# Scores and value products of the differential attention layer: from full fp32 products to three rounded ones

## What is computed

```python
def _diff_attention(cols, ...):          # 4 heads, two query/key halves of 128 features each
    qh = cols[..., :1024].reshape(b, seq, 4, 2, 128) * 128 ** -0.5
    kh = cols[..., 1024:2048].reshape(b, seq, 4, 2, 128)
    v = heads(cols[..., 2048:], 4, 256)
    for i in range(seq // 128):
        end = (i + 1) * 128
        def probs(qq, kk):
            s = einsum('bhqd,bhkd->bhqk', qq[:, :, i * 128:end], kk[:, :, :end]) + bias
            return softmax(where(mask, s, -inf))
        a = probs(q1, k1) - lam * probs(q2, k2)
        outs.append(einsum('bhqk,bhkd->bhqd', a, v[:, :, :end]))
```

## Time and profile before

| what | us |
|---|---|
| median of 3 runs (lowest, highest) | 3045.61 (3045.04, 3046.34) |
| the profiled execution, its time | 3048.35 |
| its span | 3046.6 |
| TensorE matmuls busy in the span | 3007.6 |
| VectorE busy | 2082.2 |
| ScalarE busy | 1388.7 |
| GpSimd busy | 50.6 |
| mean granted TensorE clock | 0.999 of full |

### The profile page before, as it was taken

The page is one execution under the profiler, slowest core; times in us unless marked ns, Lnnn a source line. Parts: engine busy times, 40 slices in busy tenths (PEclk is TensorE's granted clock), DMA queues, the critical chain, the costliest instruction groups (busy, mean ns, idle before and its releaser), DMA issues.

```text
span 3046.6 us, 45649 instructions
## 1 busy us (share of the span) xinstructions
PE 3007.6 (99%) x18093; PEld 2647.9 (87%) x18093; DVE 2082.2 (68%) x2423; ACT 1388.7 (46%) x1852; POOL 50.6 (2%) x148
## 2 busy tenths in 40 slices
PE   9999999999999999999999999999999999999998
PEld 8878998888888998888889988788998888889987
DVE  6987885566557876566578764656885556578854
ACT  3475553444335553344355543324553443345534
POOL 5100000000000000000000000000000000000000
PEclk9999999999999999999999999999999999999999
DMA  5122332342123333211223332223332222133322
GB/s 173 57 60 89 110 119 95 102 141 70 53 87 97 106 101 104 90 56 60 93 97 110 97 103 90 91 70 102 110 105 96 91 83 65 62 107 99 110 90 77
DMA packets 250549, 283.30 MB, mean 93 GB/s; under 512 B 11874, under 2 KB 216864, under 8 KB 250408
## 3 DMA queue, kind: packets, MB, share of 16 engines
q1 hardware_dynamic: 250408, 281.30, 28.8%
HBM read 279.16 MB, written 4.73 MB: 93 GB/s over the span
## 4 chain that ended last, share of the span: by engine, by line
PE 89%; DVE 6%; ACT 2%; issue 2%; POOL 1%; DMA 0%; SPq 0%; DVEq 0%; ACTq 0%
PE ps L2568 28%; PE ps L2203 17%; PE ps L2205 16%; PE ps L2204 16%; PE ps L2838 1%; PE ps L2840 1%; PE ps L2839 1%; PE ps L2752 1%; ACT whi L752 1%; DVE wlo L1321 1%; PE ps L2760 1%; PE ps L2819 1%; PE ps L2798 1%; PE ps L2695 1%; PE ps L2715 1%
## 5 line engine op out<-in xcount | busy, mean ns | idle before, releaser
L752 ACT ACTIVATE whi<-raw 128x2048 fp32r<-128x2048 f32 (+2 forms) x184 | 323.2, 1756 | 729.4 <-PE ps L2205 672.2
L1321 DVE TENSOR_TENSOR wlo<-raw,whi 128x2048 fp32r<-128x2048 f32 (+1 forms) x179 | 373.6, 2087 | 346.9 <-ACT whi L752 346.3
L2203 PE MATMUL ps<-hh,whi 128*128 128x512 f32 x1056 | 421.6, 399 | 0.0
L2568 PE MATMUL ps<-th,wh 128*128 128x256 f32 x1440 | 408.7, 284 | 7.3 <-ACT us L849 3.9
L2205 PE MATMUL ps<-hh,wlo 128*128 128x512 f32 x1056 | 412.0, 390 | 0.0
L2204 PE MATMUL ps<-hl,whi 128*128 128x512 f32 x1056 | 411.6, 390 | 0.0
L2568 PE MATMUL ps<-tl,wh 128*128 128x256 f32 x1440 | 407.5, 283 | 0.0
L2568 PE MATMUL ps<-th,wl 128*128 128x256 f32 x1440 | 407.4, 283 | 0.0
L2203 PE MATMUL ps<-ringh,whi 128*128 128x512 f32 x860 | 335.4, 390 | 7.5 <-issue 6.0
L2204 PE MATMUL ps<-ringl,whi 128*128 128x512 f32 x860 | 334.7, 389 | 0.0
L2205 PE MATMUL ps<-ringh,wlo 128*128 128x512 f32 x860 | 334.7, 389 | 0.0
(11 more groups left out here) (456 smaller groups left out, 5823.1 us busy)
## 6 DMA issues: line engine op xcount, KB each, us to landing
raw<-in_w_ffn_in SPq DMA_DIRECT2D x88, 1024.0 KB, 5.1
raw<-in_w_in SPq DMA_DIRECT2D x59, 1024.0 KB, 5.3
raw<-in_w_ffn_out SPq DMA_DIRECT2D x40, 1024.0 KB, 5.1
raw<-in_w_o SPq DMA_DIRECT2D x32, 640.0 KB, 4.1
raw<-in_w_gate SPq DMA_DIRECT2D x11, 1024.0 KB, 5.3
raw<-in_w_up SPq DMA_DIRECT2D x11, 1024.0 KB, 5.3
raw<-in_w_down SPq DMA_DIRECT2D x10, 1024.0 KB, 5.0
raw<-in_w_mem_kv SPq DMA_DIRECT2D x8, 1024.0 KB, 5.6
```

The costliest lines, as they stand in the source:

```text
L752: a.activation(whi[:, slot, 0:n], raw[:, slot, 0:n], ACT.Copy).then_inc(hi_made, 1)
L1321: v.tensor_tensor(wlo[:, u % 2, 0:n], raw[:, u % 2, 0:n], whi[:, u % 2, 0:n].bitcast(F32), ALU.subtract).then_inc(lo_made, 1)
L2203: mm(dst, wh, xh, start=first, stop=False, skip_group_check=True)
L2568: e = mm(bank(b, HALF), wgt[:, q, w], xx, start=start and k == 0 and m == 0, stop=k == KD // 2 - 1 and m == 2, skip_group_check=True)
```

## The change

Three things are changed.

1. Of the scores of each half, blocks 2 and 3 (384 and 512 columns) go through `three`; blocks 0 and 1 stay fp32. ScalarE makes the rounded parts of q and k (`dqk_hi`, two copies of 128x512) and VectorE the rests (`dqk_lo`, two subtractions of 128x512). Both stand at slot 2c - 2 from DZ[hd]: slot -2 for c = 0, and slot 0 for c = 1. In VectorE's program of slot 0 they stand behind the additions, maxima and negation of c = 0. TensorE waits for them (`qk_lo`) ahead of the scores.
2. Of the value products, key blocks 0 and 1 (512 and 384 columns) go through `three`. The values' first two blocks are split at slot 4 (ScalarE `dv_hi`, VectorE `dv_lo`, 512 elements a partition). At slot 5 ScalarE's one copy of 1280 columns becomes one of 384 (`dpt`) and one of 896 (`dpt_hi`), and VectorE subtracts 896 columns (`dpt_lo`) straight from PSUM. TensorE waits for `dpt_lo` and `dv_lo` ahead of the value products, and for `dpt_lo` ahead of the next head's scores.
3. Six semaphores that GpSimd sets in the first block become one, `pool_set`, with running counts. No instruction is added or removed by that.

The splits of c = 0 and the late ones lie in parts of act2's memory that are free then; those of c = 1 share dp[1]'s and dpt_hi's, so ScalarE's copies wait for the value products of the head before (`d_pv`).

```diff
@@ ScalarE, differential_slot
+                for c in range(2):
+                    for hd in at_slot(DZ, s, 2 * c - 2):
+                        act.wait_ge(acc_free, g_in(1) + evicted(2 + 3 * hd, c))
+                        act.wait_ge(S("m_tr"), 2 * MH)
+                        if hd:
+                            act.wait_ge(S("d_pv"), hd)
+                        for m, b in enumerate((qp, kp)):
+                            a.activation(dqk_hi[c][:, m, :], b[hd % 2][:, c, :], ACT.Copy).then_inc(S("qk_hi"), 1)
+                for hd in at_slot(DZ, s, 4):
+                    act.wait_ge(acc_free, g_in(1) + evicted(3 + 3 * hd, 0))
...
+                    a.activation(dv_hi[hd // 3][:, :, :], vp[hd % 2][:, 0:2, :], ACT.Copy).then_inc(S("dv_hi"), 1)
...
-                    a.activation(dpt[:, :], ps[:, 0:ZW], ACT.Copy).then_inc(S("d_pt"), 1)
+                    a.activation(dpt[:, :], ps[:, DWIDE:ZW], ACT.Copy).then_inc(S("d_pt"), 1)
+                    a.activation(dpt_hi[:, :], ps[:, 0:DWIDE], ACT.Copy).then_inc(S("d_pt"), 1)
@@ VectorE, differential_slot, behind the loop of L2028, L2032 and L2034
+                for c in range(2):
+                    for hd in at_slot(DZ, s, 2 * c - 2):
+                        for m, b in enumerate((qp, kp)):
+                            dve.wait_ge(S("qk_hi"), 2 * (NH2 + 2 * hd + c) + m + 1)
+                            v.tensor_tensor(dqk_lo[c][:, m, :], b[hd % 2][:, c, :], dqk_hi[c][:, m, :].bitcast(F32),
+                                            ALU.subtract).then_inc(S("qk_lo"), 1)
+                for hd in at_slot(DZ, s, 4):
+                    dve.wait_ge(S("dv_hi"), hd + 1)
+                    v.tensor_tensor(dv_lo[hd // 3][:, :, :], vp[hd % 2][:, 0:2, :], dv_hi[hd // 3][:, :, :].bitcast(F32),
+                                    ALU.subtract).then_inc(S("dv_lo"), 1)
+                for hd in at_slot(DZ, s, 5):
+                    dve.wait_ge(S("d_pt"), 2 * hd + 2)
+                    v.tensor_tensor(dpt_lo[hd // 3][:, :], ps[:, 0:DWIDE], dpt_hi[:, :].bitcast(F32), ALU.subtract).then_inc(S("d_ptl"), 1)
@@ TensorE, differential_slot: value products
-                    pe.wait_ge(S("d_pt"), hd + 1)
+                    pe.wait_ge(S("d_pt"), 2 * (hd + 1))
+                    pe.wait_ge(S("d_ptl"), hd + 1)
+                    pe.wait_ge(S("dv_lo"), hd + 1)
...
+                            if j < 2:
+                                three(dst, dv_hi[b][:, j, cs], dv_lo[b][:, j, cs], dpt_hi[:, keys], dpt_lo[b][:, keys], j == 0, False)
+                                continue
@@ TensorE, differential_slot: scores
+                        pe.wait_ge(S("qk_lo"), 2 * (NH2 + m + 1))
                         for i in (0, 2, 3, 1):
...
+                            if i > 1:
+                                three(dst, dqk_hi[c][:, 0, rows], dqk_lo[c][:, 0, rows], dqk_hi[c][:, 1, 0:wq(i)],
+                                      dqk_lo[c][:, 1, 0:wq(i)], i != 2, True)
+                                continue
@@ GpSimd, and its readers
-            g.memset(er[:, :, 0:1], 1.0).then_inc(S("angle_ready"), 1)
+            g.memset(er[:, :, 0:1], 1.0).then_inc(S("pool_set"), 1)
...
-                pe.wait_ge(S("t_zero"), 3)
+                pe.wait_ge(S("pool_set"), 29)
```

More of the change, by code:

```diff
@@ L429, in build @@
         dp = [at(f"dp{i}", TMP + 5120 * i, [P, ZW]) for i in range(2)]
-        dpt = at("dpt", TMP + 10240, [P, ZW])
+        DWIDE = ZK[3]
+        dpt_hi = at("dpt_hi", TMP + 10240, [P, DWIDE], F32R)
+        dpt = at("dpt", TMP + 10240 + 4 * DWIDE, [P, ZW - DWIDE])
+        LATE = [A0 + (4 + 2 * i) * 2 * T * 4 for i in range(2)]
+        dpt_lo = [at(f"dpt_lo{i}", LATE[i], [P, DWIDE], F32R) for i in range(2)]
+        dv_hi = [at(f"dv_hi{i}", LATE[i] + 3584, [P, 2, 256], F32R) for i in range(2)]
+        dv_lo = [at(f"dv_lo{i}", LATE[i] + 5632, [P, 2, 256], F32R) for i in range(2)]
+        dqk_hi, dqk_lo = ([at(f"dqk_{n}{c}", (LATE[1], TMP + 5120)[c] + 4096 * k, [P, 2, T], F32R) for c in range(2)]
+                          for k, n in enumerate(("hi", "lo")))
         osq = [at(f"osq{i}", TMP + 15360 + 2048 * i, [P, T]) for i in range(2)]
@@ L1222, in differential_slot @@
                 for c in range(2):
+                    for hd in at_slot(DZ, s, 2 * c - 2):
[7 more added lines that the diff above has]
+                    act.wait_ge(acc_free, g_in(1) + evicted(3 + 3 * hd, 0))
+                    act.wait_ge(S("m_pv"), 2 * MH)
+                    if hd:
+                        act.wait_ge(S("d_pv"), hd)
+                    if hd == 3:
+                        act.wait_ge(S("d_z"), 2 * hd + 1)
+                    a.activation(dv_hi[hd // 3][:, :, :], vp[hd % 2][:, 0:2, :], ACT.Copy).then_inc(S("dv_hi"), 1)
+                for c in range(2):
                     for hd in at_slot(DZ, s, 1 + c):
@@ L2795, in differential_slot @@
                     pe.wait_ge(acc_free, g0 + evicted(3 + 3 * hd, 1))
+                    b = hd // 3
                     for d in range(2):
                         for j in range(4):
-                            e = mm(bank(6 + d, T - P * j, P * j), vp[hd % 2][:, j, P * d:P * d + P],
-                                   dpt[:, ZK[j]:ZK[j] + wk(j)], start=j == 0, stop=j == 3, skip_group_check=True)
+                            dst, keys, cs = bank(6 + d, T - P * j, P * j), slice(ZK[j], ZK[j] + wk(j)), slice(P * d, P * d + P)
+                            if j < 2:
+                                three(dst, dv_hi[b][:, j, cs], dv_lo[b][:, j, cs], dpt_hi[:, keys], dpt_lo[b][:, keys], j == 0, False)
+                                continue
+                            e = mm(dst, vp[hd % 2][:, j, cs], dpt[:, ZK[j] - DWIDE:ZK[j] - DWIDE + wk(j)],
+                                   start=False, stop=j == 3, skip_group_check=True)
                     e.then_inc(S("d_pv"), 1)
@@ L2813, in differential_slot @@
                         elif hd:
-                            pe.wait_ge(S("d_pt"), hd)
+                            pe.wait_ge(S("d_pt"), 2 * hd)
+                            pe.wait_ge(S("d_ptl"), hd)
                         else:
@@ L2817, in differential_slot @@
                         pe.wait_ge(acc_free, g0 + evicted(2 + 3 * hd, c))
+                        pe.wait_ge(S("qk_lo"), 2 * (NH2 + m + 1))
                         for i in (0, 2, 3, 1):
-                            e = mm(ps[:, ZQ[i]:ZQ[i] + wq(i)], qp[hd % 2][:, c, P * i:P * i + P], kp[hd % 2][:, c, 0:wq(i)],
-                                   start=i != 2, stop=True, skip_group_check=True)
+                            dst, rows = ps[:, ZQ[i]:ZQ[i] + wq(i)], slice(P * i, P * i + P)
+                            if i > 1:
+                                three(dst, dqk_hi[c][:, 0, rows], dqk_lo[c][:, 0, rows], dqk_hi[c][:, 1, 0:wq(i)],
+                                      dqk_lo[c][:, 1, 0:wq(i)], i != 2, True)
+                                continue
+                            e = mm(dst, qp[hd % 2][:, c, rows], kp[hd % 2][:, c, 0:wq(i)], start=True, stop=True, skip_group_check=True)
                         e.then_inc(S("d_z"), 1)
```

34 lines of the change are left out of this document (17 added, 17 removed).

## The result

Over all runs the changed kernel takes 3058.55 us (median of 6, 3057.61 to 3062.15) and the kernel before 3046.8 (median of 6, 3045.04 to 3050.57). The ratio on record is 1.0036, with a 95% interval of 1.0026 to 1.0046 (it is not the quotient of these two medians, which lie 11.75 us or 0.39% apart): slower by 0.36%, some 11 us, where the prediction had 0.21% and a range that ended at 3056.5.

What follows compares the result with a forecast made beforehand. TensorE, busy 99% of the span, was taken as the bound. Gains, three costs and restarts summed as -4.6 + 8.6 + 1.25 + 0.7 + 0.45 = +6.4 us, giving a median of 3052.0 us (0.21% more), range 3048 to 3056.5.

Steps and rivals of the forecast that it cites:

- What bounds the kernel: TensorE, busy 99% of the span, has no slack: saved columns shorten the program, new waits lengthen it in full.
- Gains: TensorE's scores save 0.29 us in each of 8 blocks, value products 0.58 a head: -4.6 us in sum.
- Cost 1: Ahead of scores c = 1, TensorE waits 2.04 to 2.2 us a head for VectorE's late subtractions: +8.6 us.
- Cost 2: Ahead of value products, TensorE waits for dpt_lo: 0.25 us in head 0, 0.5 in heads 1 and 2; +1.25 us.
- Cost 3: At slot 6, ScalarE's copies for the next head delay the squares by 1.05 us, with 0.70 cover: +0.7 us.
- Restarts: TensorE's first product after each of nine new waits takes longer, 0.05 us each: +0.45 us.
- The clock: TensorE's granted clock was expected to stay at full behind the new waits, so the sum held no cost for it.
- Rival B: Idle times of 2.1 us drop TensorE's clock to 1.2 GHz at scores c = 1: 19 us more, 3071; chance 0.03.
- Rival A: VectorE's subtractions are ready in time at slot 1, so gains arrive without that wait: 3043.0 us; chance 0.1.
- Rival D: Value products alternate formats at a price and save nothing: 3054.3 us; chance 0.05.
- Rival C: VectorE's lateness at slot 5 reaches 1 us a head, and head 3's c = 0 is late: 3056.7; chance 0.12.
- gain bounds: Range for the summed savings in scores and value products: -2.3 to -5.5 us, value products saving 0 to 0.75 a head.

Runs made afterwards that it cites:

- e5: Changed kernel with squares, wlo and q's c = 1 subtraction reordered, k's ahead of maxima, next head's c = 0 subtractions behind addition of squares; 3046.0 us, ratio 0.9989.
- e1: Changed kernel with VectorE's two subtractions of c = 1 moved ahead of the maxima, behind the additions; 3051.04 us, ratio 1.001 to the kernel before.
- e11: Changed kernel with only wlo moved behind dv_lo and dpt_lo in slots 4 and 5 of heads 0 to 2; one run, 3056.73 us.
- e10: Changed kernel with only ScalarE's squares ahead of its copies and VectorE's addition of squares ahead of next head's subtractions and bias; one run, 3055.7 us.
- e4: Changed kernel with c = 1 subtractions ahead of maxima, squares and their addition moved up, wlo behind dv_lo and dpt_lo; 3049.76 us, ratio 1.0006.
- e2: Kernel before, products still fp32, plus two unused VectorE subtractions that TensorE waits for ahead of scores c = 1; 3061.43 us, ratio 1.0038.
- e3: Changed kernel with 18 unread TensorE transposes ahead of the wait for the subtraction of c = 1; 3057.38 us, ratio 1.0028 to the kernel before.
- e12: e5 with 14 unread TensorE transposes in the first block, ahead of head 2's scores; 3044.01 us, ratio 0.9986 to the kernel before.

## Why the prediction was wrong, point by point

**What bounds the kernel: right.** TensorE had no slack; what it was made to wait went into the time in full.

**Gains: right.** -4.6 us forecast; 0.29 a score block and 0.56 a head of value products measured in head 0, which makes -4.6 us. In e5 the stretch is 0.5 us longer than this gain and the waits left would give, so it may be a little less over all heads.

**Cost 1: the right place and size.** It had scores c = 1 come 6.78 us behind scores c = 0. They came 6.87 us behind in head 0 (1325.28 to 1332.15), where 4.64 was the undisturbed distance: 2.23 us against 2.14, over the four heads 8.8 against 8.6 us. VectorE's timeline of head 1 shows the order that does it:

```profile
1362.55 1.68 DVE L2053 TENSOR_TENSOR dp<-ps,dbias 128x128 f32<-128x128 f32 x4
1364.15 1.65 DVE L2057 TENSOR_REDUCE mx<-dp 128x1 f32<-128x128 f32 x4
1365.84 0.17 DVE L2059 TENSOR_SCALAR ngm<-mx 128x4 f32<-128x4 f32 x1
1365.92 0.68 DVE L2064 TENSOR_TENSOR dqk_lo<-qp,dqk_hi 128x512 fp32r<-128x512 f32 x1
1366.52 0.68 DVE L2064 TENSOR_TENSOR dqk_lo<-kp,dqk_hi 128x512 fp32r<-128x512 f32 x1
```

The last ends at 1367.20, and TensorE starts at 1367.35. e1 settles that this is the cause.

**Cost 2: a little too large.** 1.25 us forecast; the distance from turns to value products grew by 0.85 us in all (0.05, 0.25, 0.55 and 0), and e11 gives 0.9 back.

**Cost 3: too small by a factor of three, in part by a step left out.** 0.7 us forecast, 2.1 measured (0.8 in head 0, 1.2 in head 1, by the distances 7.46 and 7.74 from value products to the product over partitions, against 6.63 and 6.53 undisturbed, which is 7.19 and 7.08 before less 0.56). The prediction followed only ScalarE: squares 1.05 us later, cover 0.70. But on VectorE the next head's bias stands in the same slot ahead of the addition of squares, and it had been free because VectorE was waiting anyway. Now the rests hold it up. VectorE's timeline of head 1:

```profile
1391.06 0.69 DVE L2064 TENSOR_TENSOR dqk_lo<-qp,dqk_hi 128x512 fp32r<-128x512 f32 x1 [4.51 <-ACT dqk_hi L1237]
1391.67 0.68 DVE L2064 TENSOR_TENSOR dqk_lo<-kp,dqk_hi 128x512 fp32r<-128x512 f32 x1
1392.27 0.68 DVE L2038 SCALAR_TENSOR_TENSOR dbias<-dist,dneg 128x512 f32<-128x512 f32 x1
1392.99 0.69 DVE L2094 TENSOR_TENSOR osq<-osq,osq 128x512 f32<-128x512 f32 x1
```

and ScalarE's:

```profile
1391.45 1.07 ACT L1262 ACTIVATE osq<-ps 128x512 f32<-128x512 f32 x2
```

The squares end at 1392.52 and the addition starts at 1392.99: half a microsecond behind, and as much in head 0. So this step makes about 0.9 of the 2.1 us. The other 1.2 are ScalarE's lateness, which was itself forecast too small: in e10, which has the squares first, they start 4.02 and 4.04 us behind the value products, and in the changed kernel 5.18 and 5.46, so they are late by 1.2 and 1.4 us and not by 1.05. e10 moved both parts and got 1.9 us back; e4, which moved the squares and left the rests ahead of the addition, got nothing back. No run moved VectorE's part alone.

**Restarts** (0.45 us) were counted apart; the distances above hold them already.

**The clock: the step that failed.** The sum held falls at nothing; in the profiled execution two of the four long waits had one, 3.4 us in all. Rival B was given 3 in 100, against it "a wait of 1.49 us left the clock at full". Both halves of that were poor. The mechanism is real, as the changed kernel and e2 show, and e3 supports it. And that wait said little about others: it and a second one of 1.6 us in the feed-forward part have no fall behind them in any of the fourteen profiles, while the wait of 1.6 us in the first block had none in the profile of before and one in seven others. The price was also wrong, the other way: 4.7 us at each of four waits, where a fall costs 1.7 and only some waits have one. By the share seen since, as an estimate, it should have stood in the sum as 4 x 1.7 x 11/20 = 3.7 us, not beside it as 19 us at 3 in 100.

The sum in the profiled stretch: -4.6 gains, +8.8 scores, +0.85 values, +2.1 squares, +3.4 for two falls make 10.6, against 10.43 measured. Without the falls it is 7.1, against the 6.4 forecast. The median came out 6.55 us above the forecast: 3.4 of them are the two falls of the profiled execution, 0.7 the other terms, and 1.2 that the kernel before has a median of 3046.8 over six runs and had 3045.61 when the forecast was made. The last 1.2 us are not located. That falls come at some waits only would also widen the spread, which the mean clocks agree with but don't show: of the six runs of the changed kernel the two slowest, 3061.7 and 3062.2 us, have 0.996 and 0.997, the two fastest, 3057.6 and 3057.7 us, 0.998. The half clock at the end of every profiled execution, 5 to 11 us long, can alone move such a mean by 0.001.

Rival A fell: it said that the subtraction would be in time. Rival D fell with e4's block. Rival C's lateness of head 3, c = 0, did not come, and at the value products a head lost 0.55 us at most, not 1.

Two sums of the prediction are off without changing the outcome: the gain bounds -2.3 and 4 x 0.75 make -5.3, not -5.5, and 0.40 with the chances of B, C and D makes 0.60 for slower, not 0.57.

The Trainium skill ("TensorE: Matmul & The Clock Gate", "What's actually happening") says that the clock returns to 1.2 GHz after an idle window; the profiles agree in direction, with the half clock behind waits of 2 us. That such waits bring it at some times and not at others the granted clock of the changed kernel shows by itself.

## What to carry to other kernels

When a saturated engine gets work that another engine must prepare, the question is where the preparation stands in that engine's order: 0.58 us saved in a head's two score blocks was paid with 2.2 us, because two subtractions stood behind four maxima that TensorE doesn't wait for at that point. Put such a piece between what frees the buffer and what only the later steps need, and look at every instruction between the new one and the next that the saturated engine waits for, also those that were free until now. And price an idle time of TensorE of 1.6 us or more (the shortest wait that had a fall behind it here is the one of the first block) not by its length alone: add the half-clock stretch that may follow, weighted by how often it was seen in several profiles, not in one.

## What was not expected of the hardware

A wait of 1.9 to 2.1 us was followed by a stretch of 3.4 us at half clock in eleven cases of twenty, one of 1.3 to 1.5 us in none of four, and one of 3.1 to 3.3 us in three of four; which ones differs from profile to profile. The length of the wait isn't all: a wait of 1.6 us in the first block had a fall behind it in seven of thirteen profiles, and the two of 1.5 and 1.6 us in the feed-forward part (at about 550 and 615 us) in none of fourteen. With transposes that nobody reads in the wait's place the clock stayed at full in e3 (0 falls in four) and in e12's one profile. The kernel before may have the same weakness: the 27 runs of it beside e1 to e4 lie between 3044.98 and 3050.29 us; the fastest eleven have a mean clock of 0.999 each, the slowest eleven of 0.997 or 0.998. Whether that spread is the first block's fall in every case stays open, since only single executions were profiled.
